# A hybrid decoder step on one core: half of the output projection moved into the last head, and the MLP loops written out

## The reference

```python
def gdn_mixer(h, s0, conv_buf, w_in, w_conv, a_log, dt_bias, g_norm, w_out):
    proj = h @ w_in                                   # q, k, v, z, beta, decay of 8 heads
    ...                                               # causal convolution, SiLU, norms of q and k
    o, s_new = gated_delta_rule(q, k, v, g, beta, s0) # chunked recurrence, head by head
    o = o * lax.rsqrt(jnp.mean(o * o, axis=-1, keepdims=True) + EPS) * g_norm
    o = o * jax.nn.silu(z)
    out = o.reshape(N, L, VAL_W_A) @ w_out            # the output projection, 1024 x 1024
    return out, s_new, new_conv

x = x + gdn_mixer(rmsnorm(x), ...)
x = x + sq_relu_mlp(rmsnorm(x), w_up, w_down)         # 1024 -> 4096 -> 1024
```

## Time and profile before

| | us |
|---|---|
| median of 3 runs | 3006.82 |
| the three runs | 3007.53, 3001.81, 3006.82 |
| the profiled execution's own time | 3001.38 |
| its span, first to last instruction | 2999.6 |
| TensorE busy in it | 2837.3 |
| VectorE, ScalarE, GpSimd busy | 1622.5, 857.3, 71.9 |

### The profile page before, as it was taken

One profiled execution on the slowest core, in us unless ns is written; L12 is line 12 of the kernel. 1 busy time (PEld: TensorE's weight loads), 2 busy tenths in 40 slices (PEclk: granted clock), 3 DMA queues, 4 the chain that ended last, 5 costly groups with the idle time before them and its releaser, 6 DMA issues.

```text
span 2999.6 us, 46264 instructions
## 1 busy us (share of the span) xinstructions
PE 2837.3 (95%) x18460; PEld 2750.6 (92%) x18460; DVE 1622.5 (54%) x2956; ACT 857.3 (29%) x1914; POOL 71.9 (2%) x94
## 2 busy tenths in 40 slices
PE   4999999999886999999999999999799999999998
PEld 2999999999864999999999999997599999999997
DVE  4766777667435354444444464556765444444445
ACT  3544444444222222111121131333442211112111
POOL 0000000000020000000000000000320000000000
PEclk8999999999776999999999999999899999999999
DMA  3100110002103011111111123433311111111111
GB/s 117 46 20 30 36 37 24 22 30 92 65 36 131 23 49 57 42 42 42 56 42 42 56 72 102 119 96 114 122 44 50 49 42 42 43 55 42 47 38 57
DMA packets 81363, 170.22 MB, mean 57 GB/s; under 512 B 21369, under 2 KB 46241, under 8 KB 80884
## 3 DMA queue, kind: packets, MB, share of 16 engines
q1 hardware_dynamic: 72868, 154.93, 15.6%
q10 hardware_dynamic: 8352, 13.28, 1.3%
HBM read 136.69 MB, written 36.73 MB: 58 GB/s over the span
## 4 chain that ended last, share of the span: by engine, by line
PE 90%; DVE 5%; DMA 2%; issue 1%; ACT 1%; SPq 0%; POOL 0%; ACTq 0%; DVEq 0%; POOLq 0%
PE psum L1930 18%; PE psum L1931 18%; PE psum L1932 18%; PE psum L2139 6%; PE psum L2032 4%; PE psum L2033 4%; PE psum L2034 4%; PE psum L1957 3%; PE psum L2375 2%; PE psum L2353 2%; PE psum L2311 1%; PE psum L2312 1%; PE psum L2313 1%; PE psum L2199 1%; PE psum L2169 1%
## 5 line engine op out<-in xcount | busy, mean ns | idle before, releaser
L1930 PE MATMUL psum<-x_hi,w_hi 128*128 128x352 f32 (+1 forms) x1120 | 362.2, 323 | 10.8 <-DVE w_lo L1045 7.3
L1931 PE MATMUL psum<-x_lo,w_hi 128*128 128x352 f32 (+1 forms) x1120 | 359.1, 321 | 0.0
L1932 PE MATMUL psum<-x_hi,w_lo 128*128 128x352 f32 (+1 forms) x1120 | 357.3, 319 | 0.0
L1045 DVE SCALAR_TENSOR_TENSOR w_lo<-w_raw,gains,w_hi 128x512 fp32r<-128x512 f32 x384 | 267.2, 753 | 63.0 <-ACT w_hi L556 62.7
L556 ACT ACTIVATE w_hi<-w_raw,gains 128x512 fp32r<-128x512 f32 x384 | 249.6, 712 | 142.5 <-DMA w_raw<-in_w 130.7
L2032 PE MATMUL psum<-x_hi,w_hi 128*128 128x352 f32 (+1 forms) x768 | 273.1, 356 | 13.2 <-issue 10.7
L1930 PE MATMUL psum<-x_hi_b,w_hi 128*128 128x352 f32 (+1 forms) x768 | 247.1, 322 | 3.4 <-DVE x_b L1556 3.1
L2033 PE MATMUL psum<-x_lo,w_hi 128*128 128x352 f32 (+1 forms) x768 | 247.7, 323 | 0.0
L2034 PE MATMUL psum<-x_hi,w_lo 128*128 128x352 f32 (+1 forms) x768 | 247.4, 322 | 0.0
L1930 PE MATMUL psum<-u_hi_b,w_hi 128*128 128x352 f32 (+1 forms) x768 | 246.7, 321 | 0.0
L1930 PE MATMUL psum<-u_hi,w_hi 128*128 128x352 f32 (+1 forms) x768 | 246.3, 321 | 0.0
(11 more groups left out here) (333 smaller groups left out, 5800.1 us busy)
## 6 DMA issues: line engine op xcount, KB each, us to landing
w_raw<-in_w SPq DMA_DIRECT2D x192, 512.0 KB, 3.6
q_tile<-scratch_q SPq DMA_DIRECT2D x24, 256.0 KB, 3.0
scratch_att<-o_out ACTq DMA_DIRECT2D x32, 132.0 KB, 2.4
x<-in_x SPq DMA_DIRECT2D x8, 516.0 KB, 8.4
scratch_o_heads<-head_out ACTq DMA_DIRECT2D x8, 512.0 KB, 2.7
s_state<-in_s_rec_in ACTq DMA_DIRECT2D x2, 2048.0 KB, 10.0
out_s_rec<-s_state SPq DMA_DIRECT2D x8, 512.0 KB, 2.6
o_raw<-scratch_o_heads SPq DMA_DIRECT2D x8, 512.0 KB, 7.5
```

The source lines that it names most:

```text
L1045: done = v.scalar_tensor_tensor(w_lo[:, slot, 2 * part + k], w_raw[:, part, k], gains[:, bass.ds(unit * UW + 2 * part + k, 1)], f(w_hi[:, ...
L1930: mm(out, whi, xh[:, k, cols], start=k == 0, stop=False)
L1931: mm(out, whi, xl[:, k, cols], start=False, stop=False)
L1932: done = mm(out, wlo, xh[:, k, cols], start=False, stop=k == kts - 1)
```

## The change

The change does five things:

- **Two halves.** The output projection is cut over its input features. The half with heads 0 to 3 (24 products of 4 steps, 96 steps) is issued from level 5 of head 7 on, by `early`; the half with heads 4 to 7 follows after the last head. The weight units are reordered in the host's packing, so that the first half has slots 0 and 1 and the second half slots 2 and 3.
- **Loads.** Heads 0 to 3 are loaded into `o_in` (the lower half of `x_lo`) as soon as `x_lo` is no longer read, together with a fresh copy of x (`x_half`, the upper halves of `x_hi` and `x_lo`). The sums of the early products go into this copy, the later products add it into x. `x_back` is gone. Heads 4 to 6 are loaded during head 7's recurrence, head 7's output is taken from where it lies.
- **Splits.** ScalarE makes the high parts of heads 0 to 3 between levels 3 and 4 of head 7, VectorE the low parts at the end of level 4.
- **Samples.** PSUM banks 0 and 1 now belong to the early products, so the samples use bank 2 alone. The 64 state reads are cut in two (after levels 1 and 2), the 8 pairs of updates into 16 single ones (from level 4 on).
- **MLPs.** The six blocks of each MLP are written out on TensorE, VectorE and ScalarE, without a loop.

```diff
+def early_done(place):
+
+    return max(place + 1, 0) if place < 4 else min(4 + 68 * (place - 3) // 24, 72)
...
+    half = UW * NT * 4
+    o_in = at("o_in", [P, UW, NT], F32, [x_start + KT * NT * 4, region])
+    x_half = [at(f"x_half{n}", [P, UW, NT], F32, [x_start + n * KT * NT * 4 + half, region]) for n in range(2)]
...
+    later = [pairs[0][:, 0], pairs[0][:, 1], low[:].rearrange("p c n -> p (c n)"),
+             head_out[:].rearrange("p c n -> p (c n)")]
...
+        for part in range(2):
+            weight(U_OUT + 2, part)
...
+        sp.wait_ge(sem("product_free"), L.next("product_free", 12 * HEADS))
+        L.skip("product_free", -12 * HEADS)
+        sp.wait_ge(sem("head_output_stored"), L.next("head_output_stored", 16 * (HEADS - 1)))
+        for k in range(UW):
+            sp.dma_start(o_in[:, k, 0:SEQ], t["o_heads"][:, k]
+            ).then_inc(sem(f"o{k}_landed"), L.add(f"o{k}_landed", 16))
+        for n in range(2):
+            sp.dma_start(x_half[n][:], t["x"][:, UW * n:UW * n + UW]).then_inc(sem("x_reloaded"), L.add("x_reloaded", 16))
+        sp.wait_ge(sem("state_ready"), L.next("state_ready", HEADS))
+        for k in range(3):
+            sp.dma_start(later[k], t["o_heads"][:, UW + k]
+            ).then_inc(sem(f"o{UW + k}_landed"), L.add(f"o{UW + k}_landed", 16))
...
-        sp.wait_ge(sem("head_output_stored"), L.next("head_output_stored", 16 * HEADS))
+        for part in range(2):
+            weight(U_OUT + 3, part)
...
-        for k in range(KT):
-            sp.dma_start(o_raw[:, k], t["o_heads"][:, k]
-            ).then_inc(sem(f"o_raw{k}_landed"), L.add(f"o_raw{k}_landed", 16))
-        stream(U_OUT + 2, U_KVQ + 2)
+        stream(U_MLP0, U_KVQ + 2)
...
+                    for k in range(UW):
+                        act.wait_ge(sem(f"o{k}_landed"), L.next(f"o{k}_landed", 16))
+                        act.activation(x_hi[:, k, 0:SEQ], o_in[:, k, 0:SEQ], ACT.Copy
+                        ).then_inc(sem("o_hi_ready"), L.add("o_hi_ready"))
...
+        def output_hi(k, cols):
+            act.activation(x_hi[:, k, cols], later[k][:, cols], ACT.Copy).then_inc(sem("o_hi_ready"), L.add("o_hi_ready"))
+        act.wait_ge(sem("product_free"), L.next("product_free", 16))
+        for k in range(3):
+            act.wait_ge(sem(f"o{UW + k}_landed"), L.next(f"o{UW + k}_landed", 16))
+            output_hi(k, first)
         act.wait_ge(sem("s_state_stored"), L.next("s_state_stored", 16 * HEADS))
         split_hi(U_OUT + 2, 2)
+        act.wait_ge(sem("head_out_ready"), L.next("head_out_ready"))
+        output_hi(3, first)
+        act.wait_ge(sem("product_free"), L.next("product_free", 8))
+        for k in range(UW):
+            output_hi(k, rest)
         split_hi(U_OUT + 3, 3)
...
-        def samples_update(n):
-
-            if n:
-                old = s_state[(n - 1) // 4][:, (n - 1) % 4]
+        def samples_update(u):
+
+            n, h = divmod(u, 2)
+            old = s_state[n // 4][:, n % 4, hc(h)]
+            if h == 0:
                 v.wait_ge(sem("s_scaled_ready"), L.next("s_scaled_ready"))
-                for h in range(2):
-                    v.wait_ge(sem(f"s_update{h}_full"), L.next(f"s_update{h}_full"))
-                    v.tensor_tensor(old[:, hc(h)], old[:, hc(h)], psum[:, 1 + h].rearrange("p (c n) -> p c n", n=P), ALU.add
-                    ).then_inc(sem("s_state_ready" if h else "dve_order"), L.add("s_state_ready" if h else "dve_order"))
+            v.wait_ge(sem(f"s_update{h}_full"), L.next(f"s_update{h}_full"))
+            if h:
+                v.wait_ge(sem("s_half_ready"), L.value("s_half_ready"))
+            mark = "s_state_ready" if h else "s_half_ready"
+            v.tensor_tensor(old, old, psum[:, 2].rearrange("p (c n) -> p c n", n=P), ALU.add).then_inc(sem(mark), L.add(mark))
...
+        def early_product(n):
+            third, tile = divmod(n, 8)
+            if n == 0:
+                v.wait_ge(sem("x_reloaded"), L.next("x_reloaded", 32))
+            out = x_half[tile // UW][:, tile % UW, THIRDS[third]]
+            v.wait_ge(sem("product_full"), L.next("product_full"))
+            v.tensor_tensor(out, out, psum[:, n % 2, 0:width(third)], ALU.add
+            ).then_inc(sem("product_free"), L.add("product_free"))
+
+        def output_low(k, src, cols):
+            v.wait_ge(sem("o_hi_ready"), L.next("o_hi_ready"))
+            v.tensor_tensor(x_lo[:, k, cols], src[:, cols], f(x_hi[:, k, cols]), ALU.subtract
+            ).then_inc(sem("o_split"), L.add("o_split"))
...
+                if last and level > 4:
+                    early_products(2 * level - 10)
+                    samples_update(2 * level - 9)
...
+                if last and level == 4:
+                    for k in range(UW):
+                        output_low(k, o_in[:, k], slice(0, SEQ))
...
+        early_products(28)
         out_scale()
+        for k in range(3):
+            output_low(k, later[k], first)
+        split_lo(U_OUT + 2, 2)
+        early_product(18)
+        early_product(19)
         out_gate()
-
-
-        def x_back(k):
-            v.tensor_tensor(x[:, k], f(x_hi[:, k]), f(x_lo[:, k]), ALU.add).then_inc(sem("x_back"), L.add("x_back"))
-        x_back(0)
-        for k in range(KT):
-            if k + 1 < KT:
-                x_back(k + 1)
-            v.wait_ge(sem("o_hi_ready"), L.next("o_hi_ready"))
-            v.tensor_tensor(x_lo[:, k, 0:SEQ], o_raw[:, k], f(x_hi[:, k, 0:SEQ]), ALU.subtract
-            ).then_inc(sem("o_split"), L.add("o_split"))
-        v.tensor_copy(x_hi[:, :, SEQ:], s_og[:]).then_inc(sem("dve_order"), L.add("dve_order"))
-        v.wait_ge(sem(L.last), L.value(L.last))
-        v.tensor_tensor(x_lo[:, :, SEQ:], s_og[:], f(x_hi[:, :, SEQ:]), ALU.subtract
-        ).then_inc(sem("samples_ready"), L.add("samples_ready"))
+        early_product(20)
+        output_low(3, later[3], first)
+        for n in range(21, 24):
+            early_product(n)
+        for k in range(UW):
+            output_low(k, later[k], rest)
+        output_samples(1)
...
-            with L.loop(6, name) as b:
+            for b in range(6):
                 up(unit + 4 + 4 * b)
                 down(unit + 4 + 4 * b)
...
+                if last and level < 3:
...
+                    for n in range(32 * level - 32, 32 * level):
+                        mm(psum[:, 2, 128 + 2 * n:130 + 2 * n], s_state[n // 32][:, n // NS % 4, n % NS], s_u[:, 0:2, n],
...
+        def early(a, b):
+
+            for m in range(a, b):
+                n, k = divmod(m, UW)
+                third, tile = divmod(n, 8)
+                if m == 0:
+                    pe.wait_ge(sem("raw_free"), L.next("raw_free", 4))
+                    pe.wait_ge(sem("o_split"), L.next("o_split", UW))
+                    L.skip("product_free", 1)
+                if n == 16 and k == 0:
+                    pe.wait_ge(sem("samples_ready"), L.next("samples_ready"))
+                if k == 0:
+                    pe.wait_ge(sem("product_free"), L.next("product_free"))
+                whi = w_hi[:, tile // UW, k, tile % UW * P:(tile % UW + 1) * P]
+                wlo = w_lo[:, tile // UW, k, tile % UW * P:(tile % UW + 1) * P]
+                out, cols = psum[:, n % 2, 0:width(third)], THIRDS[third]
+                mm(out, whi, x_hi[:, k, cols], start=k == 0, stop=False)
+                mm(out, whi, x_lo[:, k, cols], start=False, stop=False)
+                done = mm(out, wlo, x_hi[:, k, cols], start=False, stop=k == UW - 1)
+                if k == UW - 1:
+                    done.then_inc(sem("product_full"), L.add("product_full"))
...
+                if last:
+                    early(early_done(place + 3), early_done(place + 4))
...
+                if last and c < 6:
+                    samples_update(2 * c + 5)
...
+        early(72, 80)
         out_turned()
-
-        L.skip("product_free", -3)
-        pe.wait_ge(sem("raw_free"), L.next("raw_free", 4))
-        first_products((0, 1), "o_split")
-        pe.wait_ge(sem("raw_free"), L.next("raw_free", 4))
+        early(80, 96)
+
+        pe.wait_ge(sem("product_free"), L.next("product_free", 2))
+        L.skip("product_free", -6)
+        pe.wait_ge(sem("raw_free"), L.next("raw_free", 2))
+        first_products(2, "o_split")
...
-            with L.loop(6, name):
+            for _ in range(6):
                 up()
                 down()
```

174 lines of the change are left out of this document (91 added, 83 removed).

## The result

The changed kernel takes 2951.7 us (median of four runs, 2947.9 to 2957.7) against 3006.5 us for the kernel before on the same chip (3001.8 to 3007.5): ratio 0.9821, 95% interval 0.9808 to 0.9833. The forecast was 2953 us, with 2932 to 2978 as its range. The profiled execution is the longest of the four, 2957.68 us with a span of 2955.7; that of before was the shortest of its own, so the spans differ by only 43.9 us where the medians differ by 54.8.

A forecast was written before the change was run, and what follows sets the result against it. TensorE, busy 95% of the span, was taken as the bound, so gains lie in its idle stretches or clock. Terms +10 - 7 + 8 - 52 - 10.7 = -51.7 us gave 2955.1, taken as 2953, range 2932 to 2978.

The forecast's parts named there:

- the likeliest case: Whole kernel: the forecast's own case, with 2943 to 2963 us as its range; chance 0.56.
- Loads: Head 7's state load beside new loads of o_in and x: +10 us as middle, between nothing lost and +19.
- The sentence on the Trainium skill's rule: State load: DMA engines take turns between queues with work, so the state lands after 8.4 MB, +12.7 us.
- Reads: Head 7's state reads, cut in two with the same 64 matmuls: 27.4 us stay.
- Levels: Head 7's levels 4 to 6, end of level 3 to recurrence: 28.8 us, that is -7; ends -14 and +6.
- Recurrence: Head 7's recurrence with early steps and 11 updates: 53.8 us against 45.7, +8; ends +6 and +58.
- Rival A: Clock stays at 1.2 GHz through head 7; recurrence 50 us over forecast, levels some 10 more: 3013 us; chance 0.05.
- failure mode that was cited beside A: Early products: cycling PSUM banks with small idle times between matmul groups keeps dropping the clock; they use only two banks.
- After the recurrence: Recurrence's end to layer A's end: 71 us against 122.8, -52; ends -60 and -42.
- Both bared waits: TensorE waits about 4.6 us for a PSUM bank after the recurrence, 5 more for the MLP's first weight splits.
- Loops: MLP loops written out: 5.35 us saved per MLP, -10.7 for both; other end 0.
- Rival B: Written-out MLP loops give nothing, through code fetching or VectorE's last additions: +10.7, about 2964 us; chance 0.12.

The follow-up runs named there:

- experiment 2: Changed kernel with the loads of o_in and x_half waiting until both halves of s_state have landed: 2949.5 us, ratio 0.9811 to the kernel before.
- Experiment 5: Changed kernel with all 64 pairs of s_state read together behind level 1: 2954.4 us, ratio 0.9826 to the kernel before.
- experiment 8: Changed kernel with loads held, VectorE reordered, MLP splits earlier: 2932.3 us; also with ScalarE's copies and VectorE's subtractions of heads 0 to 3 in level 2: 2929.5 us.
- Experiments 3 and 4: Each on the changed kernel: VectorE takes products 18 and 19 right after output scaling, 2942.2 us; MLP's first two weight splits one third earlier, 2942.3 us.
- experiment 1: Kernel before with MLP loops written out: on TensorE, ScalarE and VectorE 2996.5 us; TensorE alone 2995.3 us; ScalarE and VectorE alone 3006.0 us.

## Why the prediction was right, and where its terms were off

The forecast, 2953 us, was right to 1.3 us, and the likeliest case, with its own range, was what happened. That it was so near is in part luck: the sum itself came to 2955.1, the 2 us between have no reason given, and the errors of the terms partly cancel. The terms, in its order:

**Loads, +10 forecast: +3.8 measured.** The small matmuls ahead of the state's load come 0.7 us earlier than before (L2219 at 789.94, before at 790.61), so the sharing itself cost 4.5. The step that failed is "So 4.2 MB took 12.7 us, 330 GB/s" as the rate for the shared engines. The 12.7 us hold some 2.9 in which no full stream runs; while data flowed, the one queue moved 427 GB/s and the two moved 426 (experiment 2). By that rate the upper end would be +15 and my middle +7 (an estimate from these rows). The rest is the share: 2.35 of q1's 6.3 MB went before the state was complete, not half. The first of my ends, "if the state still went first", was not the case either: from the small matmuls to the reads it takes 12.6 to 13.3 us with held loads and 15.2 to 17.1 with shared ones, in three and six kernels. The sentence on the Trainium skill's rule gave +12.7 by the same rate of 330 and by equal bytes of both queues. The same page of the Trainium skill, DMA: Bandwidth & Descriptors, section on queues, rings and completion order, says that the turn goes by packets. The trace shows that the bytes were not shared equally, and that the queue with the smaller packets got fewer. It does not show turns of one packet each: q1 sent 585 of the profile's packets while q10 sent 288.

**Reads, 0 forecast: -4.3.** The step "with the same 64 matmuls, so 27.4 us" took the clock for given. Experiment 5 showed that level 2 between the halves brings it up. Levels 2 and 3 gave 2.4 of it back: without the reads they took 17.8 us, not 15.4 (830.66 to 846.09 before), since their own clock was lower (0.74 from 836.87 to 848, 0.82 from 836.6 to 846.1 before) and the small samples' matmuls waited 2.3 us for VectorE, not 1.6. The split moves the slow stretch more than it removes it.

**Levels, -7 forecast: -7 measured.** From the end of level 3 (847.95) to the recurrence 28.8 us. The waits inside were smaller, 2.6 for 3.6 and 1.5 for 2; a wait of 1.35 us for VectorE's clearing of the state, with GpSimd's preparation in the chain, made up for it. The forecast took the right number of updates here, one in level 4 and two each in levels 5 and 6; the kernel before has four pairs ahead of the recurrence. Moving the copies (experiment 8) took the first two away.

**Recurrence, +8 forecast: +11.2.** The mis-sized part is the updates, "11 updates of 0.97". Chunks 2 to 5 take (916.65 - 885.77) / 4 = 7.7 us, the last two, without updates, 5.0. That is 1.36 per update, 4.3 us over all; the chunks without came out 0.1 to 0.2 us shorter than the 5.14 forecast. The first chunk was 9.0 us long, with the slow start in it. Rival A, half clock throughout, did not come: 1.00 from 886 to 934. It named a real mechanism all the same. With no early steps the clock is 0.51, so A's ground is what these steps keep away. Two PSUM banks in turn did no harm to the clock, so no run here shows the failure mode that was cited beside A.

**After the recurrence, -52 forecast: -50.3** (71 forecast, 73.0 measured by this edge, which includes the last addition; TensorE's first matmul of the MLP comes 71.4 us behind the recurrence). Both bared waits came where they were forecast and as large: 4.4 for 4.6, 4.7 for 5. Experiments 3 and 4 removed each by its named cause, and won 6.8 and 7.2 us. The difference to the waits is the half-speed spells, 4.9 us together where the forecast had 3.5.

**Loops, -10.7 forecast: -8.4 to -10.5** by the medians, -10.2 by the traces (5.1 for each MLP). By the blocks it is 0.86 each where 0.95 was taken. Rival B is refuted by the kernels of experiment 1. That TensorE's own loop is the cause had not been said; experiment 1 shows it, but not whether it is the branch or the wait at it.

The errors partly cancel: -6.2 and -4.3 at the state, against +2.4 in levels 2 and 3, +3.2 in the recurrence and +1.7 after it. Layer A's end was forecast 41 us earlier and came 44.1 earlier.

## What to carry to other kernels

When a stretch of dependent work runs at half clock, independent matmuls put into it may be nearly free. Here 68 steps cost 6.5 us where 72 cost 32 behind it, because the full clock that they bring pays them back. It pays where the stretch has long matmuls of its own: the chunks with two updates grew by 0.2 us, those without by 1.3. So cost them by the chunk at both clocks and not by the idle time. And after work has been moved ahead, look at once at what VectorE and ScalarE do around the seam: in this case more than half of the remaining gain (22 us) was theirs, in waits of 4 to 5 us that each brought a slow spell along.

## What the runs showed of the hardware that was not expected

- A hardware loop on TensorE cost 0.86 us a round, branch and wait for the last matmul together, and the trace gave as its releaser VectorE, whose own loop could be written out without effect.
- Reads of 2 columns gain from the clock as well: 32 of them (two records each, x64 in the view) took 13.79 us at 0.50, 10.36 at 0.67, 9.34 at 0.75 and 8.73 at 0.81. Time multiplied by clock is 6.9 to 7.1 in all four.
- Two DMA queues together moved 426 GB/s, and one alone moved 427 while its data flowed. A transfer of 4.2 MB lost 2 to 4.5 us to 6.3 MB issued beside it in smaller packets.
- Half-speed spells followed both waits of 4 to 5 us: each was worth 2.4 to 2.5 us on top of its wait.
